# Squares of the residual added on GpSimd, one ones product in place of eight

## The chip, the cores and the metric

One core of a Trainium2 chip runs the whole program in one launch. The metric is the device time in microseconds, the median of repeated runs. The tensor engine (PE in the profile, its weight loads PEld), VectorE (DVE), ScalarE (ACT), GpSimd (POOL) and the DMA queue of SyncE (SP) run side by side and meet at semaphores.

## The reference

A residual x of 256 tokens by 1024 features, float32, goes through ten stages. Each takes a normed copy of x, puts it through a mixer or a feed-forward network, and adds the outcome to x:

```python
def rms_norm(x, gain):
    xf = x.astype(jnp.float32)
    y = xf * lax.rsqrt(jnp.mean(xf * xf, axis=-1, keepdims=True) + NORM_EPS)
    return (y * gain.astype(jnp.float32)).astype(x.dtype)
...
    for l in range(DEPTH):
        h = rms_norm(x, attn_norm[l])
        x = x + hybrid_mixer(h, ...)
        h = rms_norm(x, ffn_norm[l])
        x = x + conv_ffn(h, ...)
```

The first block above has two layers, so four stages: hybrid, ffn1, hybrid, ffn1. The second block has six: ffn2, a short convolution, ffn2, ffn2, a gated delta rule, ffn2. In those six the outcome of a stage is normed as well before it is added: `h = h + rms_norm_2(mix, g[3])`. The mean of squares over the 1024 features of each token, at the head of every stage, is what this case is about.

## The kernel before

**Layout.** Features lie on the 128 partitions: x is one SBUF tile `x` of 128 x 8 x 256, eight feature tiles (`KT`) of 256 tokens each. All weights come as 623 panels of 128x1024 float32, from HBM through a ring of six buffers `raw` (SyncE's queue). ScalarE rounds each panel to `whi` (line 762), VectorE subtracts to get the low part `wlo` (L1113), and the tensor engine makes each float32 product from three: high by high, high by low, low by high (`mm3`, L1701 to L1703). x is split in the same way to `xhi` (ScalarE, L778) and `xlo` (VectorE, L1124). Each panel is one call of `up` or `down`: 24 such products of 256 columns.

**Between two stages** everything goes tile by tile over k = 0 to 7. VectorE's `finish` updates x: from a bank in one operation where the stage has no norm behind it (L1152 after a hybrid, L1159 after ffn1), in two where it has (a scaled copy `tmp` from the bank, L1155, and `x<-x,tmp`, L1157). Two tiles behind it, it makes the `xlo` of the next stage (`prepare_tile`). ScalarE's `prepare` squares each tile to one of four buffers `sq` (L777) and makes its `xhi`; from the fifth tile on it waits with each square until the buffer has been read. The tensor engine's `up` is called with `prepare` for the first panel of a stage: for each k it waits for `xlo`, runs the three products, waits for the square and runs the ones product (L1721). This product, a matrix of ones by `sq` in plain float32, adds over the partitions and broadcasts the sum to all of them; the eight accumulate in `bank[6]`. In the delta stage that panel is the one of the gates.

**Behind the eighth ones product** VectorE takes mean and epsilon (`ms`, L1131), ScalarE the root (L781), VectorE the reciprocal (`rstd`, L1133). `rstd` is applied to the results of the panels, so the tensor engine needn't wait for it: it has two panels ready at the boundary, three where the stage has a norm behind it (`lead`). Further panels are split by VectorE only after `rstd`.

**GpSimd** does little. In stage 0 it issues ten loads (L681 and L686: tables, masks, and the small weights `w_in`, `pos_in`, `gate_w_in`), in stage 2 it issues four of them again as soon as stage 0 has released the space, and it has some products in the hybrid (L711, L714) and delta stages (L731, L737, L746). VectorE waits for the small weights before the copy at L1293, at the second tile of a hybrid stage. `third` is a pair of 128x256 buffers for the blocks of a stage, free at the boundaries.

Of the kernel before, what the change touches and what calls it, by code (L numbers as in the profile page):

```python
# [6 lines left out]
S = 256  # L7
KT = D // P
# [9 lines left out]
ALU = mybir.AluOpType  # L18
# [261 lines left out]
def build(nc, stages, arrays):  # L280
# [14 lines left out]
    with ExitStack() as ctx:  # L295
        def sb(name, shape, dt=F32):
            return ctx.enter_context(nc.sbuf_tensor(name, shape, dt))

        def sem(name):
            return ctx.enter_context(nc.semaphore(name))  # L300

        bank = [ctx.enter_context(nc.psum_tensor(f"bank{i}", [P, 512], F32)) for i in range(8)]
# [8 lines left out]
        ones = sb("ones", [P, P])  # L311
# [3 lines left out]
        sq = sb("sq", [P, 4, S])  # L315
# [7 lines left out]
        first = sb("first", [P, 2, S + 2])  # L323
        second = sb("second", [P, 2, S])
        third = sb("third", [P, 2, S])
        conv = sb("conv", [P, 2, S])
        act_out = sb("act_out", [P, 2, S])
        h = sb("h", [P, 2, S])
# [142 lines left out]
        xhi_ready = sem("xhi_ready")  # L471
        xlo_ready = sem("xlo_ready")
        sum_ready = sem("sum_ready")
        ms_ready = sem("ms_ready")
        root_ready = sem("root_ready")
        rstd_ready = sem("rstd_ready")
# [186 lines left out]
        def _(pool):  # L663
# [5 lines left out]
            def hybrid(s):  # L669
# [32 lines left out]
                for li in range(NL - 1):  # L702
# [9 lines left out]
                    if li == 0:  # L712

                        pool.tensor_tensor(level_k[0], gqk[:, 2:4, :], decay_, ALU.mult).then_inc(y["qe_ready"], 1)  # L714

            for s in range(n_stages):
                if stages[s][0] == HYBRID:
                    hybrid(s)
                if stages[s][0] != DELTA:
# [32 lines left out]
        def _(act):  # L752
# [16 lines left out]
            def prepare(s):  # L769

                for k in range(KT):
                    n = s * KT + k
                    wait_x(act, s, k)
                    if n >= 4:

                        act.wait_ge(sum_ready, n - 3)
                    act.activation(sq[:, n % 4, :], x[:, k, :], ACT.Square).then_inc(sq_ready, 1)  # L777
                    act.activation(xhi[:, k, :], x[:, k, :], ACT.Copy, scale=col(("pre", s), k)) \  # L778
                        .then_inc(xhi_ready, 1)
                act.wait_ge(ms_ready, s + 1)  # L780
                act.activation(rt[:], ms[:], ACT.Sqrt).then_inc(root_ready, 1)  # L781
# [317 lines left out]
        def _(dve):  # L1099
# [27 lines left out]

            def prepare_rstd(s):

                dve.wait_ge(sum_ready, KT * (s + 1))  # L1130
                dve.tensor_scalar(ms[:], bank[6][:, S:2 * S], 1.0 / D, EPS, ALU.mult, ALU.add).then_inc(ms_ready, 1)  # L1131
                dve.wait_ge(root_ready, s + 1)
                dve.reciprocal(rstd[:], rt[:]).then_inc(rstd_ready, 1)  # L1133
                dve.wait_ge(rstd_ready, s + 1)
# [563 lines left out]
        def _(pe):  # L1698
# [6 lines left out]
            def up(s, p, turn, dst, prepare=None):  # L1705

                slot = p % RING

                pe.wait_ge(lo_done, used(p, turn))
                for k in range(KT):  # L1710
                    if prepare is not None:

                        pe.wait_ge(xlo_ready, prepare * KT + k + 1)
                    last = mm3(dst, whi[slot][:, k * P:(k + 1) * P], wlo[slot][:, k * P:(k + 1) * P],
                               xhi[:, k, :], xlo[:, k, :], k == 0, k == KT - 1)
                    if k == KT - 1:
                        last.then_inc(panel_used, 1)
                    if prepare is not None:
                        n = prepare * KT + k
                        pe.wait_ge(sq_ready, n + 1)  # L1720
                        pe.matmul(bank[6][:, S:2 * S], ones[:], sq[:, n % 4, :], start=(k == 0), stop=(k == KT - 1),  # L1721
                                  skip_group_check=True).then_inc(sum_ready, 1)

            def down(s, f, p, turn):

# [496 lines left out]
```

## Time and profile before

| | us |
|---|---|
| median of 3 timed runs | 2488.87 (2486.8 to 2492.01) |
| span of the profiled execution, first to last instruction | 2484.9 |
| tensor engine busy | 2270.0 |
| weight loads busy | 2202.7 |
| VectorE busy | 1552.0 |
| ScalarE busy | 1107.8 |
| GpSimd busy | 76.6 |
| mean granted clock of the tensor engine | 0.958 |

The profile is of one execution, of which only the span is known; the median of the timed runs is 4.0 us above it. Weight loads overlap the products. A matmul's duration in the profile overlaps that of its neighbours, so the pace of a stream is read from starts. The granted clock is 1 at 2.4 GHz and 0.5 at 1.2 GHz.

### The profile page before, as it was taken

The page shows a single profiled execution, that of the slowest core. Times are in us where ns is not written, and L with a number is a line of the kernel's source. Part 1 is how long each engine was busy: PE and PEld are TensorE (multiplying, and loading weights), DVE is VectorE, ACT ScalarE, POOL GpSimd, SP SyncE. Part 2 cuts the span into 40 slices and gives each one's busy share as a digit, 9 for nine tenths or more (in the row PEclk, how much of TensorE's full clock was granted, in tenths as well). Part 3 has the DMA queues.
Part 4 walks back from the last instruction along what each step waited for, and adds up shares of the span by engine and source line. Part 5 has one row for each costly group of instructions (what it writes and reads, how often), then busy time and mean ns, then how long its engine had stood idle before and what let it go on. Part 6 is the DMA issues. An engine that isn't in the chain of part 4 may idle for free.

```text
span 2484.9 us, 46837 instructions
## 1 busy us (share of the span) xinstructions
PE 2270.0 (91%) x18150; PEld 2202.7 (89%) x18150; DVE 1552.0 (62%) x2543; ACT 1107.8 (45%) x1762; POOL 76.6 (3%) x84
## 2 busy tenths in 40 slices
PE   7998999999999999999898998998586877898997
PEld 6978999989789999999898998998576876898997
DVE  4456777754577777665677656665575655566665
ACT  4443455544444555544445445444424233245443
POOL 1002000000020000000000000000011010000000
PEclk9899999998999999999999999999788989999999
DMA  7432455543324455555354553553211111053552
GB/s 233 141 102 85 152 190 196 184 130 108 101 87 153 164 191 185 170 178 191 129 189 144 177 189 128 191 186 127 83 37 51 35 52 43 1 170 127 198 182 76
DMA packets 92186, 339.06 MB, mean 136 GB/s; under 512 B 10672, under 2 KB 10872, under 8 KB 91552
## 3 DMA queue, kind: packets, MB, share of 16 engines
q1 hardware_dynamic: 90288, 329.61, 39.7%
q0 software_dynamic: 1776, 7.73, 1.2%
q8 instruction: 89, 1.46, 0.2%
q14 instruction: 33, 0.27, 0.0%
HBM read 334.67 MB, written 2.62 MB: 136 GB/s over the span
## 4 chain that ended last, share of the span: by engine, by line
PE 79%; DVE 12%; ACT 6%; issue 3%; POOL 0%; DMA 0%; DVEq 0%; SPq 0%; ACTq 0%; POOLq 0%
PE bank L1701 22%; PE bank L1703 21%; PE bank L1702 21%; PE bank L2065 6%; DVE wlo L1113 3%; ACT whi L762 2%; DVE conv L1501 2%; PE bank L1721 1%; PE bank L1851 1%; PE bank L1777 1%; DVE arena L1285 1%; DVE tmp L1155 1%; ACT conv L968 1%; PE bank L1911 1%; DVE prstd L1145 0%
## 5 line engine op out<-in xcount | busy, mean ns | idle before, releaser
L1701 PE MATMUL bank<-xhi,whi 128*128 128x256 f32 x3496 | 1023.4, 293 | 82.9 <-DVE xlo L1124 50.7
L1702 PE MATMUL bank<-xlo,whi 128*128 128x256 f32 x3496 | 992.2, 284 | 0.0
L1703 PE MATMUL bank<-xhi,wlo 128*128 128x256 f32 x3496 | 991.6, 284 | 0.0
L1113 DVE TENSOR_TENSOR wlo<-raw,whi 128x1024 fp32r<-128x1024 f32 x623 | 741.4, 1231 | 245.5 <-ACT whi L762 245.1
L1701 PEld LDWEIGHTS bank<-xhi,whi 128*128 128x128 f32 x3496 | 674.4, 193 | 103.2 <-issue 66.7
L1702 PEld LDWEIGHTS bank<-xlo,whi 128*128 128x128 f32 x3496 | 674.1, 193 | 3.0
L1703 PEld LDWEIGHTS bank<-xhi,wlo 128*128 128x128 f32 x3496 | 671.9, 192 | 0.0
L762 ACT ACTIVATE whi<-raw 128x1024 fp32r<-128x1024 f32 x623 | 622.8, 1046 | 53.1 <-DVE arena L1282 21.6
L1701 PE MATMUL bank<-hhi,whi 128*128 128x256 f32 x1376 | 391.8, 285 | 7.1 <-DVE hlo L1234 5.6
L1703 PE MATMUL bank<-hhi,wlo 128*128 128x256 f32 x1376 | 390.3, 284 | 0.0
L1702 PE MATMUL bank<-hlo,whi 128*128 128x256 f32 x1376 | 390.0, 283 | 0.0
L1701 PEld LDWEIGHTS bank<-hhi,whi 128*128 128x128 f32 x1376 | 263.7, 192 | 8.8 <-issue 8.8
L1703 PEld LDWEIGHTS bank<-hhi,wlo 128*128 128x128 f32 x1376 | 264.0, 192 | 0.0
L1702 PEld LDWEIGHTS bank<-hlo,whi 128*128 128x128 f32 x1376 | 263.9, 192 | 0.0
L803 ACT ACTIVATE act_out<-first 128x256 f32<-128x256 f32 x104 | 43.6, 419 | 392.5 <-DVE first L1213 349.0
L2065 PE MATMUL bank<-arena 128*128 128x128 f32 x1184 | 147.9, 284 | 29.2 <-ACT arena L1027 14.5
L2065 PEld LDWEIGHTS bank<-arena 128*128 128x128 f32 x1184 | 141.6, 198 | 35.0 <-ACT arena L1027 15.7
L1213 DVE TENSOR_TENSOR first<-bank,rstd 128x256 f32<-128x256 f32 x132 | 55.8, 423 | 177.3 <-PE bank L1703 176.9
L821 ACT ACTIVATE hhi<-h 128x256 fp32r<-128x256 f32 x172 | 71.9, 418 | 146.8 <-DVE h L1232 92.9
L1234 DVE TENSOR_TENSOR hlo<-h,hhi 128x256 fp32r<-128x256 f32 x156 | 66.3, 425 | 75.5 <-ACT hhi L821 75.5
L1232 DVE TENSOR_TENSOR h<-act_out,second 128x256 f32<-128x256 f32 x148 | 63.0, 426 | 42.4 <-ACT act_out L812 21.6
L871 ACT ACTIVATE arena<-arena 128x256 f32<-128x256 f32 x48 | 20.0, 417 | 136.7 <-DVE arena L1285 136.7
(320 smaller groups left out, 1950.5 us busy)
## 6 DMA issues: line engine op xcount, KB each, us to landing
raw<-panels SPq DMA_DIRECT2D x623, 512.0 KB, 4.2
arena<-w_in POOLq DMA_DIRECT2D x2, 2048.0 KB, 10.6
bias_table<-arena POOLq DMA_DIRECT2D x1, 1536.0 KB, 34.1
x<-x_in SPq DMA_DIRECT2D x1, 1024.0 KB, 4.9
arena<-bias_table POOLq DMA_DIRECT2D x1, 1024.0 KB, 9.9
out<-x SPq DMA_DIRECT2D x1, 1024.0 KB, 3.9
masks<-masks_in SPq DMA_DIRECT2D x1, 576.0 KB, 6.0
arena<-level_masks_in POOLq DMA_DIRECT2D x1, 512.0 KB, 7.6
```

What stands on the lines that cost most here:

```text
L762: act.activation(whi[slot][:], raw[slot][:], ACT.Copy).then_inc(hi_done, 1)
L803: act.activation(act_out[:, sl, :], first[:, sl, 2:], ACT.Silu).then_inc(act_done, 1)
L821: act.activation(hhi[:, sl, :], h[:, sl, :], ACT.Copy).then_inc(hhi_done, 1)
L1113: dve.tensor_tensor(wlo[slot][:], raw[slot][:], whi[slot][:].bitcast(F32), ALU.subtract) \
L1213: dve.tensor_tensor(first[:, sl, 2:], pair[:, 0:S], rstd[:], ALU.mult).then_inc(gate_scaled, 1)
L1232: dve.tensor_tensor(h[:, sl, :], gated[:, sl, :], second[:, sl, :], ALU.mult).then_inc(h_done, 1)
L1234: dve.tensor_tensor(hlo[:, sl, :], h[:, sl, :], hhi[:, sl, :].bitcast(F32), ALU.subtract) \
L1501: last = dve.scalar_tensor_tensor(out=conv[:, sl, :], in0=delta_in[:, sl, w:w + S], scalar=col(("tap", s), w * 4 * KH + t), in1=conv[:, sl ...
L1701: pe.matmul(dst, w_hi, a_hi, start=start, stop=False, skip_group_check=True)
L1702: pe.matmul(dst, w_hi, a_lo, start=False, stop=False, skip_group_check=True)
L1703: return pe.matmul(dst, w_lo, a_hi, start=False, stop=stop, skip_group_check=True)
L2065: last = pe.matmul(bank[out_bank][:, m * P:(m + 1) * P], lhs(m), rhs(m), start=True, stop=True)
```

## The change

GpSimd gets a function `add_squares`, which it runs at the head of its work for each stage: seven additions that sum the eight squares to `sq_sum`, the first half of `third`. Each waits for its square and for the addition before it, the first also for the ones product of the stage before. ScalarE's squares wait for these additions instead of for ones products. The tensor engine runs one ones product on the sum, after the 24 products of the first panel, and VectorE waits for that one.

```diff
+        sq_sum = third[:, 0, :]
...
+        added = sem("added")
...
+            def add_squares(s):
+
+                if s:
+                    pool.wait_ge(sum_ready, s)
+                for k in range(1, KT):
+                    pool.wait_ge(sq_ready, KT * s + k + 1)
+                    if k > 1:
+                        pool.wait_ge(added, (KT - 1) * s + k - 1)
+                    a = sq[:, 0, :] if k == 1 else sq_sum
+                    pool.tensor_tensor(sq_sum, a, sq[:, k % 4, :], ALU.add).then_inc(added, 1)
+
             for s in range(n_stages):
+                add_squares(s)
                 if stages[s][0] == HYBRID:
                     hybrid(s)
...
-                    if n >= 4:
-
-                        act.wait_ge(sum_ready, n - 3)
+                    if k >= 4:
+
+                        act.wait_ge(added, (KT - 1) * s + max(k - 4, 1))
+                    elif s:
+
+                        act.wait_ge(added, (KT - 1) * s)
                     act.activation(sq[:, n % 4, :], x[:, k, :], ACT.Square).then_inc(sq_ready, 1)
...
-                dve.wait_ge(sum_ready, KT * (s + 1))
+                dve.wait_ge(sum_ready, s + 1)
...
-                    if prepare is not None:
-                        n = prepare * KT + k
-                        pe.wait_ge(sq_ready, n + 1)
-                        pe.matmul(bank[6][:, S:2 * S], ones[:], sq[:, n % 4, :], start=(k == 0), stop=(k == KT - 1),
-                                  skip_group_check=True).then_inc(sum_ready, 1)
+                if prepare is not None:
+
+                    pe.wait_ge(added, (KT - 1) * (prepare + 1))
+                    pe.matmul(bank[6][:, S:2 * S], ones[:], sq_sum, start=True, stop=True,
+                              skip_group_check=True).then_inc(sum_ready, 1)
```

GpSimd's order at the start of the program, before (loads are marked DMA; the semaphore waited for stands in brackets):

```order
L664 MEMSET ones 128x128
L665 MEMSET first 128x2x2
L681 DMA rel_table<-rel_in 32x8 [waits masks_loaded]
L681 DMA arena<-onehot_in 32x384
L681 DMA arena<-masked_in 8x384
L681 DMA arena<-level_masks_in 128x1024
L681 DMA arena<-cmp_masks_in 128x240
L681 DMA halves<-halves_in 128x2
L686 DMA arena<-w_in 128x4096
L686 DMA arena<-w_in 128x128
L686 DMA arena<-pos_in 128x32
L686 DMA arena<-gate_w_in 16x256
```

and with the change, whose lines are shifted by 2:

```order
L666 MEMSET ones 128x128
L667 MEMSET first 128x2x2
L727 ISA
L727 TENSOR_TENSOR third<-sq 128x256 [waits sq_ready,masks_loaded]
L727 TENSOR_TENSOR third<-third,sq 128x256 [waits added,sq_ready] x6
L683 DMA rel_table<-rel_in 32x8
L683 DMA arena<-onehot_in 32x384
L683 DMA arena<-masked_in 8x384
L683 DMA arena<-level_masks_in 128x1024
L683 DMA arena<-cmp_masks_in 128x240
L683 DMA halves<-halves_in 128x2
L688 DMA arena<-w_in 128x4096
```

The seven additions stand ahead of all ten loads. In stage 2 the four loads of L686 also stand behind that stage's additions now, where they had followed stage 0's products directly.

The tensor engine's first panel of a stage before, its first three tiles:

```order
L1701 MATMUL bank<-xhi,whi 128x256 [waits lo_done,xlo_ready,masks_loaded,consts_ready]
L1702 MATMUL bank<-xlo,whi 128x256
L1703 MATMUL bank<-xhi,wlo 128x256
L1721 MATMUL bank<-sq,ones 128x256 [waits sq_ready]
L1701 MATMUL bank<-xhi,whi 128x256 [waits xlo_ready]
L1702 MATMUL bank<-xlo,whi 128x256
L1703 MATMUL bank<-xhi,wlo 128x256
L1721 MATMUL bank<-sq,ones 128x256 [waits sq_ready]
```

and with the change:

```order
L1718 MATMUL bank<-xhi,whi 128x256 [waits lo_done,xlo_ready,masks_loaded,consts_ready]
L1719 MATMUL bank<-xlo,whi 128x256
L1720 MATMUL bank<-xhi,wlo 128x256
L1718 MATMUL bank<-xhi,whi 128x256 [waits xlo_ready]
L1719 MATMUL bank<-xlo,whi 128x256
L1720 MATMUL bank<-xhi,wlo 128x256
```

The ones product and its wait are gone from between the triples; one of each stands behind the eighth.

## Rows read from the trace of the kernel before

**Rows 1.** The page: busy time, share and instructions of each engine.
```profile
PE 2270.0 (91%) x18150; PEld 2202.7 (89%) x18150; DVE 1552.0 (62%) x2543; ACT 1107.8 (45%) x1762; POOL 76.6 (3%) x84
```
**Rows 2.** View of line 1721, the ones products: durations in ns, first and last start.
```profile
L1721 PE MATMUL bank<-sq,ones x160: 377/379/634, 15.3 to 2282.6; 128*128 128x256 f32 x160
```
**Rows 3.** Timeline of PE, stage 1: start, us, idle before and its releaser.
```profile
320.31 0.60 PE L1721 MATMUL bank<-sq,ones 128*128 128x256 f32 x2
...
321.10 0.59 PE L1721 MATMUL bank<-sq,ones 128*128 128x256 f32 x2
...
325.82 0.59 PE L1721 MATMUL bank<-sq,ones 128*128 128x256 f32 x2
...
330.43 0.39 PE L1701 MATMUL bank<-xhi,whi 128*128 128x256 f32 x1 [1.19 <-DVE wlo L1113]
```
**Rows 4.** Timeline of DVE, the boundary into stage 1.
```profile
317.88 1.08 DVE L1152 SCALAR_TENSOR_TENSOR x<-bank,x 128x256 f32<-128x256 f32 x3
...
320.71 0.47 DVE L1124 SCALAR_TENSOR_TENSOR xlo<-x,cols,xhi 128x256 fp32r<-128x256 f32 x1
...
321.44 0.48 DVE L1124 SCALAR_TENSOR_TENSOR xlo<-x,cols,xhi 128x256 fp32r<-128x256 f32 x1
...
324.28 0.48 DVE L1124 SCALAR_TENSOR_TENSOR xlo<-x,cols,xhi 128x256 fp32r<-128x256 f32 x1 [0.28 <-ACT xhi L778]
326.45 0.42 DVE L1131 TENSOR_SCALAR ms<-bank 128x256 f32<-128x256 f32 x1 [1.69 <-PE bank L1721]
```
**Rows 5.** Timeline of PE, the first panel of stage 5.
```profile
1214.41 0.55 PE L1701 MATMUL bank<-xhi,whi 128*128 128x256 f32 x1 [5.93 <-DVE xlo L1124]
...
1222.66 0.59 PE L1721 MATMUL bank<-sq,ones 128*128 128x256 f32 x2
```
**Rows 6.** Timeline of DVE, the boundary into stage 5.
```profile
1216.29 0.48 DVE L1124 SCALAR_TENSOR_TENSOR xlo<-x,cols,xhi 128x256 fp32r<-128x256 f32 x1
...
1217.54 0.48 DVE L1124 SCALAR_TENSOR_TENSOR xlo<-x,cols,xhi 128x256 fp32r<-128x256 f32 x1
...
1221.10 0.48 DVE L1124 SCALAR_TENSOR_TENSOR xlo<-x,cols,xhi 128x256 fp32r<-128x256 f32 x1 [0.18 <-ACT xhi L778]
1223.29 0.42 DVE L1131 TENSOR_SCALAR ms<-bank 128x256 f32<-128x256 f32 x1 [1.71 <-PE bank L1721]
```
**Rows 7.** Line 737 in ns; POOL and DVE near 1817; the page's L1113.
```profile
L737 POOL TENSOR_TENSOR arena<-tmp,arena x16: 724/1171/1707, 1816.5 to 2114.6; 128x256 f32<-128x256 f32 x16
...
1817.47 1.17 POOL L737 TENSOR_TENSOR arena<-tmp,arena 128x256 f32<-128x256 f32 x1
...
1816.85 2.34 DVE L1620 TENSOR_TENSOR arena<-arena,masks 128x512 f32<-128x512 f32 x2
1819.12 1.75 DVE L1113 TENSOR_TENSOR wlo<-raw,whi 128x1024 fp32r<-128x1024 f32 x1
...
L1113 DVE TENSOR_TENSOR wlo<-raw,whi 128x1024 fp32r<-128x1024 f32 x623 | 741.4, 1231 | 245.5 <-ACT whi L762 245.1
```
**Rows 8.** Windows: stretch, us; busy PE (x), others; PEclk, DMA share, GB/s.
```profile
1214.40:1218.70 4.30, 4.29 (x16) 3.85 (x16) 4.16 (x11) 2.77 (x7) 0.00 (x0) 0.50 0.02 4
...
1223.00:1229.00 6.00, 6.00 (x52) 5.97 (x51) 5.19 (x5) 4.22 (x5) 0.00 (x0) 1.00 0.08 21
...
1823.50:1828.50 5.00, 3.30 (x15) 0.50 0.03 13
```
**Rows 9.** The start: POOL, ACT and DVE; L686's loads, min/median/max to landing.
```profile
8.02 0.69 POOL L681 DMA_DIRECT2D rel_table<-rel_in  x1 [7.02 <-DMA masks<-masks_in]
...
11.35 1.06 POOL L686 DMA_DIRECT2D arena<-w_in  x2
...
13.01 0.40 ACT L777 ACTIVATE sq<-x 128x256 f32<-128x256 f32 x1
...
31.10 0.66 DVE L1293 COPY arena<-tmp 128x240 f32<-128x240 f32 x2
...
DMA to landing us min/median/max: 7.8/10.5/12.9
```

## The prediction

> **What bounds the kernel now.** I read the page's busy line first. The tensor engine is busy for 2270.0 of 2484.9 us and GpSimd for 76.6 us [rows 1]: one engine bounds, and another is nearly free. The view of the line with the ones products comes next. Its 160 records are 80 products, since a plain float32 product leaves two records [rows 2]. Then I read the timelines of two of the ten places where a stage prepares its residual, because every product that goes stands there.
>
> Stage 1 stands for stages 1 to 4, which follow a stage without a norm behind it. The ones products start every 0.79 us (320.31, 321.10), the last at 325.82 [rows 3]. A dense triple takes 0.35 us, three times 6.00/51 [rows 8], so one ones product costs 0.44 us. VectorE makes the low parts xlo at a faster pace, one in 0.73 us (320.71, 321.44); the last ends at 324.76 and the mean square starts at 326.45, 1.69 us later [rows 4]. Here the tensor engine is the slower of the two, by little. Afterwards it waits for VectorE again, 1.19 us at 330.43 [rows 3].
>
> Stage 5 stands for stages 5 to 9, which follow a stage with a norm behind it. VectorE needs 1.25 us per tile (1216.29, 1217.54), its last xlo ends at 1221.58, and the mean square starts at 1223.29, 1.71 us later [rows 6]. The tensor engine came out of 5.93 us of idleness [rows 5], and its granted clock was 0.50 for the first 4.3 us of this work, 1.2 of 2.4 GHz [rows 8]. VectorE sets the pace, and the ones products fill time that the tensor engine would wait out.
>
> **What goes.** 70 of 80 products at 0.44 us are 31 us of tensor time. On the path lies only what the engine trails behind xlo. With the ones products out of the loop, the mean square would follow the last xlo by a triple, one ones product and some 0.25 us of handing over: 1.04 us at full clock instead of 1.7, or 1.8 us at half clock (0.70 + 0.88 + 0.25).
>
> **What comes: seven adds on GpSimd.** The nearest row is its multiply of 128x256 tiles: 0.72 us at best, median 1.17, at most 1.71 [rows 7]. A chain of seven with a wait of some 0.06 us each takes 5.5 us undisturbed, 8.6 us at the median. It cannot end before the last square, but where squares come every 1.25 us it keeps up.
>
> The dearer part is what these adds do to VectorE. Around 1817 both engines work on pairs of SBUF tiles, and they alternate: each GpSimd multiply takes 1.17 us, and two VectorE operations take 2.34 us [rows 7]. The split of a panel right behind them took 1.75 us against a mean of 1.23 [rows 7], so one GpSimd operation held it up by 0.52 us; I take 0.55. The Trainium skill, "SBUF — State Buffer", section "Who interferes with whom", says that the second of the two engines is blocked for the whole instruction of the first, and only if VectorE reads two SBUF tiles; with 0.72 us per block the term for stages 5 to 9 below would be 0.54 us per tile and the sum some 5 us more.
>
> In stages 1 to 4 the xlo operation reads x and xhi, two SBUF tiles; the update reads a bank and can run under an add. The cycle becomes 0.55 + 0.33 = 0.88 us instead of 0.73: over seven tiles the last xlo is **1.1 us** later. The adds, in step with it, end earlier. In stages 5 to 9 an add meets two such operations per tile (x<-x,tmp and xlo), and hides only the 0.18 us or so by which it overlaps the scaled copy from the bank: 0.37 us more per tile, six times, **2.2 us**. Both bounds are open: 0 if nothing is blocked, 0.55 for each of eight tiles (4.4 us) if every add blocks in full.
>
> **The clock.** Around 1826 the tensor engine was busy for 3.30 of 5.00 us at half clock and was not granted more [rows 8]. In stages 5 to 9 a triple at half clock (0.70 us) now falls into a cycle of some 1.6 us, without the ones products between them, so I expect half clock until the dense work begins with the last triple. If the return takes 4.3 us as above, 1.5 us of it is priced in the 1.8 us above, and the other 2.8 us does half of its work: **1.4 us** lost, since the engine has panels ready there (0.9 to 2.5 by how the return falls). In stages 1 to 4 a full-clock triple fills 0.35 of 0.88 us, and the clock may fall too. Then the handing over takes 1.8 us instead of 1.7, and the next panel is slower by more than the 1.19 us wait hides; together 0.2 us. The Trainium skill, "TensorE: Matmul & The Clock Gate", Part 1, calls the throttled clock the default, which activity releases; so it speaks against taking filler products away.
>
> **The start.** GpSimd's queue now has the seven adds ahead of its ten loads. The second square is there at 13.41 [rows 9]; seven adds at 0.88 us end near 19.7. Six loads take 3.3 us to issue (8.02 to 11.35), so w_in is issued near 23.0 and its three followers by 24.6. With 7.8 to 12.9 us to landing, all are there at 32.4 to 37.5. VectorE needs them for the copy that stands at 31.10 [rows 9]. The mean square itself comes earlier by 1 to 2 us, as squares no longer wait for ones products, but this wait eats it. VectorE's next splits and reads stand behind the wait, and the tensor engine behind them. I take the early landing, since the panels' own first rush is over by then: **+1.5 us** (-1.5 to +6). For stage 2 the loads are issued near 522 instead of 314. With 7.9 us they land just before the copy at 531; I cost this at nothing, and 3 us if landing takes 12.9.
>
> **Sum.** Stages 1 to 4: 1.1 + 0.2 = 1.3, four times 5.2. Stages 5, 6, 7, 9: 2.2 + 1.4 = 3.6, four times 14.4. Stage 8: 2.2, the tensor engine waits for VectorE there afterwards in any case. The start: 1.5. Together +23.3. The profiled span is 2484.9 and the median of the timed runs 2488.87, so 4.0 lies around it: 2484.9 + 23.3 + 4.0 = **2512 us**, 0.9% slower. The chance is 0.50.
>
> **Rivals.**
> 1. GpSimd's chain is the bound, at its median of 1.17 us plus the wait. In stages 1 to 4 seven adds end 8.6 us after the second square instead of 6.2, which makes the mean square 1.6 us later still (four times: 6.4), and the start 2.4 us later. 2512 + 8.8 = 2521. For it: the median is what it needs beside a busy VectorE. Against it: VectorE's pairs here are 256 wide, those at 1817 were 512. 0.20.
> 2. The loads are late, 12.9 us to landing at the start and at stage 2: 4.5 + 3 more, 2520. 0.10.
> 3. The blocking is small, and only the clock bites: without the 1.1 and 2.2 us, stages 1 to 4 give about nothing, four of the others 1.4, the start 1.5: +7, 2496. Against it stands the split of 1.75 us. 0.12.
> 4. The other side: neither blocking nor clock. Then the mean square comes 0.65 us earlier at nine places, and the start gains 1.5: -7.4, 2481. It decides once the last xlo slips by less than 0.65 us and the clock is full by the last triple. The clock speaks against it: with less work between idle gaps it would have to return sooner. 0.03.
> 5. Gains and losses cancel to within 0.2%, which is 5 us and about what a measurement can tell from no change: parts of 3 and 4 mixed. 0.05.
>
> **How the numbers follow.** The range runs from rival 3 at its low end to rival 1 together with late loads: 2496 to 2532. Outside it are rivals 4 and 5, and mishaps above. Faster 0.03, same 0.09 (rival 5 and the low third of rival 3), slower 0.88.
>
> **What would show it.** VectorE's x<-x,tmp and xlo operations, now 0.42 and 0.48 us, must show longer ones while adds run, and the last xlo of stage 5 must end 12 to 13 us after the first update instead of 10.4. Granted clock 0.50 until behind the ones product there. A wait before the copy of the start. If xlo keeps its pace, the first term falls; if the clock returns as before, the 1.4 us falls; if the tensor engine waits for GpSimd behind the last triple, rival 1 holds. A time under 2494 would make the whole argument wrong.

## The result and the profile after

| | before | changed |
|---|---|---|
| median of the timed runs | 2489.74 us (2486.8 to 2492.01, 4 runs) | 2515.97 us (2513.16 to 2518.97, 4 runs) |
| span of the profiled execution | 2484.9 | 2511.4 |
| mean granted clock | 0.958 | 0.942 |

The ratio is 1.0102, with an interval of 1.0086 to 1.0117: 26.2 us slower. In a later set of runs on another chip it was 1.0088 (1.0074 to 1.0103), some 22 us.

The page's busy line of the changed kernel, as [rows 1]:

```profile
PE 2281.7 (91%) x18010; PEld 2207.5 (88%) x18010; DVE 1572.5 (63%) x2543; ACT 1108.3 (44%) x1762; POOL 129.1 (5%) x154
```

140 matmul records are gone, and yet the tensor engine is busy 11.7 us longer: the rest runs at a colder clock. GpSimd has 70 operations and 52.5 us more. VectorE has not one operation more and is busy 20.5 us longer. The views of the adds, of the update behind a norm and of xlo, in ns (min/median/max), first and last start, forms:

```profile
L727 POOL TENSOR_TENSOR third<-third,sq x60: 725/732/858, 14.9 to 2305.4; 128x256 f32<-128x256 f32 x60
...
L1174 DVE TENSOR_TENSOR x<-x,tmp x48: 424/438/721, 1217.0 to 2506.7; 128x256 f32<-128x256 f32 x48
...
L1141 DVE SCALAR_TENSOR_TENSOR xlo<-x,cols,xhi x80: 472/617/953, 14.1 to 2305.8; 128x256 fp32r<-128x256 f32 x80
```

The adds run at 0.73 us. The two VectorE operations that read two SBUF tiles have stretched: the update was never over 0.43 us before, and xlo had a median of 0.48. The operations that read one bank and one SBUF tile kept their 0.41 and 0.48 us. The adds themselves, six of stage 3:

```profile
818.17 5.11 POOL L727 TENSOR_TENSOR third<-third,sq 128x256 f32<-128x256 f32 x6
```

They start every 0.876 us ((5.11 - 0.73)/5): 0.73 us of add and 0.14 us of handing over from each to the next, with no wait for a square.

**Stage 1**, the timeline of DVE in the changed kernel, answers to [rows 4]:

```profile
318.83 0.42 DVE L1169 SCALAR_TENSOR_TENSOR x<-bank,x 128x256 f32<-128x256 f32 x1
319.16 0.62 DVE L1141 SCALAR_TENSOR_TENSOR xlo<-x,cols,xhi 128x256 fp32r<-128x256 f32 x1
319.70 0.41 DVE L1169 SCALAR_TENSOR_TENSOR x<-bank,x 128x256 f32<-128x256 f32 x1
320.04 0.62 DVE L1141 SCALAR_TENSOR_TENSOR xlo<-x,cols,xhi 128x256 fp32r<-128x256 f32 x1
...
322.67 1.88 DVE L1141 SCALAR_TENSOR_TENSOR xlo<-x,cols,xhi 128x256 fp32r<-128x256 f32 x3
326.51 0.42 DVE L1148 TENSOR_SCALAR ms<-bank 128x256 f32<-128x256 f32 x1 [1.97 <-PE bank L1738]
```

xlo starts every 0.88 us (319.16, 320.04) where it was 0.73, the pace of the adds. Each is issued while an add runs and ends some 0.28 us after it. In stages 2 to 4 the last two, with no update between them, take 0.95 us each. The wait behind the last one is 1.97 us, not 1.69. The timeline of PE there answers to [rows 3]:

```profile
319.38 0.28 PE L1720 MATMUL bank<-xhi,wlo 128*128 128x256 f32 x1
...
320.71 0.58 PE L1718 MATMUL bank<-xhi,whi 128*128 128x256 f32 x1 [0.26 <-DVE xlo L1141]
321.10 0.41 PE L1719 MATMUL bank<-xlo,whi 128*128 128x256 f32 x1
...
325.42 1.05 PE L1738 MATMUL bank<-third,ones 128*128 128x256 f32 x2
```

After two or three triples with gaps between them a product takes 0.41 us instead of 0.28, half clock, and so does the one ones product.

**Stage 5**, the timelines of POOL and of DVE, the latter for [rows 6]:

```profile
1221.43 0.74 POOL L727 TENSOR_TENSOR third<-third,sq 128x256 f32<-128x256 f32 x1 [0.81 <-ACT sq L794]
1222.97 0.74 POOL L727 TENSOR_TENSOR third<-third,sq 128x256 f32<-128x256 f32 x1 [0.81 <-ACT sq L794]
```

```profile
1221.22 0.47 DVE L1172 SCALAR_TENSOR_TENSOR tmp<-bank,cols,prstd 128x256 f32<-128x256 f32 x1
1221.72 0.72 DVE L1174 TENSOR_TENSOR x<-x,tmp 128x256 f32<-128x256 f32 x1
1222.37 0.47 DVE L1141 SCALAR_TENSOR_TENSOR xlo<-x,cols,xhi 128x256 fp32r<-128x256 f32 x1
...
1228.04 0.71 DVE L1141 SCALAR_TENSOR_TENSOR xlo<-x,cols,xhi 128x256 fp32r<-128x256 f32 x1 [0.16 <-ACT xhi L795]
1230.71 0.42 DVE L1148 TENSOR_SCALAR ms<-bank 128x256 f32<-128x256 f32 x1 [1.96 <-PE bank L1738]
```

The add of 1221.43 ends at 1222.17; the update issued at 1221.72 ends 0.27 us after that, 0.30 us late. The xlo behind it meets no add and takes 0.47. That is so for the four tiles in the middle; the first and the last xlo meet an add and take 0.95 and 0.71 us, so 0.47 + 4 x 0.30 + 0.23 makes the 1.9 us by which the last xlo is late. The windows of the changed kernel (busy time of PE, PEld, DVE, ACT and POOL, PEclk, DMA share, GB/s), as [rows 8]:

```profile
1220.00:1228.00 8.00, 5.47 (x17) 4.03 (x18) 7.71 (x17) 4.09 (x11) 3.95 (x6) 0.50 0.00 0
1228.50:1234.50 6.00, 6.00 (x38) 5.82 (x37) 3.52 (x4) 3.33 (x5) 0.00 (x0) 0.72 0.00 0
```

Half clock lasts through the loop and well into the dense work behind it.

**Where the time went**, by stage, in us, worked out from the start of the first update, the end of the last xlo, and the starts of the mean square and of the next stage's first update; changed less before, profile against profile:

| stage | to the last xlo | from there to the mean square | from there to the next stage | sum |
|---|---|---|---|---|
| 0 (hybrid) | -0.22 | +0.52 | -1.13 | -0.8 |
| 1 | +0.61 | +0.28 | 0.00 | +0.9 |
| 2 (hybrid) | +1.08 | +0.27 | +1.28 | +2.6 |
| 3 | +1.09 | +0.27 | 0.00 | +1.4 |
| 4 | +1.07 | +0.24 | -0.07 | +1.2 |
| 5 | +1.87 | +0.25 | +0.44 | +2.6 |
| 6 | +1.86 | +0.27 | +0.59 | +2.7 |
| 7 | +1.88 | +0.28 | +1.24 | +3.4 |
| 8 (delta) | +1.65 | +0.27 | +7.37 | +9.3 |
| 9 | +1.88 | +0.28 | +1.05 | +3.2 |

Together 26.5. The 7.37 us in the delta stage stand where no line of the change does.

### The profile page after: what moved, and what is told of

Its sections match the earlier page's. It is cut to its first block, busy times and chain, and to the rows that moved or that the text cites. A ratio compares the mean times of both kernels' runs of the same rounds, so it can differ in the third digit from the quotient of the medians.

```text
span 2511.4 us, 46697 instructions
## 1 busy us (share of the span) xinstructions
PE 2281.7 (91%) x18010; PEld 2207.5 (88%) x18010; DVE 1572.5 (63%) x2543; ACT 1108.3 (44%) x1762; POOL 129.1 (5%) x154
## 4 chain that ended last, share of the span: by engine, by line
PE 78%; DVE 13%; ACT 5%; issue 3%; POOL 0%; DMA 0%; DVEq 0%; SPq 0%; ACTq 0%; POOLq 0%
PE bank L1718 22%; PE bank L1719 21%; PE bank L1720 21%; PE bank L2082 6%; DVE wlo L1130 3%; ACT whi L776 2%; DVE conv L1518 2%; DVE xlo L1141 1%; PE bank L1868 1%; PE bank L1794 1%; DVE tmp L1172 1%; DVE arena L1302 1%; ACT conv L985 1%; PE bank L1928 1%; PE bank L2199 0%
## 5 line engine op out<-in xcount | busy, mean ns | idle before, releaser
L1719 PE MATMUL bank<-xlo,whi 128*128 128x256 f32 x3496 | 1002.4, 287 | 0.0
L1718 PEld LDWEIGHTS bank<-xhi,whi 128*128 128x128 f32 x3496 | 682.7, 195 | 127.8 <-issue 69.5
L1719 PEld LDWEIGHTS bank<-xlo,whi 128*128 128x128 f32 x3496 | 685.3, 196 | 1.0
L1720 PEld LDWEIGHTS bank<-xhi,wlo 128*128 128x128 f32 x3496 | 682.6, 195 | 0.0
L2082 PEld LDWEIGHTS bank<-arena 128*128 128x128 f32 x1184 | 143.3, 200 | 34.9 <-ACT arena L1044 15.7
L727 POOL TENSOR_TENSOR third<-sq 128x256 f32<-128x256 f32 x10 | 8.1, 814 | 1419.8 <-ACT sq L794 1419.8
```

Of the source, the lines that this page charges most:

```text
L1718: pe.matmul(dst, w_hi, a_hi, start=start, stop=False, skip_group_check=True)
L1719: pe.matmul(dst, w_hi, a_lo, start=False, stop=False, skip_group_check=True)
L1720: return pe.matmul(dst, w_lo, a_hi, start=False, stop=stop, skip_group_check=True)
L2082: last = pe.matmul(bank[out_bank][:, m * P:(m + 1) * P], lhs(m), rhs(m), start=True, stop=True)
```

## The experiments

Nine other kernels ran, and the two once more. "Table" below means the same division by stage, against before's first profile.

**The adds alone**: all eight ones products stay, and GpSimd sums the squares for nobody.

```diff
+            for s in range(n_stages):
+                add_squares(s)
...
+                dve.wait_ge(added, (KT - 1) * (s + 1))
```

> The kernel before with the seven GpSimd adds put in, whose sum nobody reads; the eight ones products stay in the loop. Blocking theory: the last xlo ends 8.0 us after the first update at stages 1 to 4 (before: 6.9) and 12.2 us at stages 5 to 9 (before: 10.35), with the ones products the tensor engine stays at full clock, so the mean square follows the last xlo by 1.0 to 1.1 us instead of 1.7; net +0.4 us at four places and +1.2 us at five, about +8 us in all, 2498. Rival, only the lost ones products cost (clock): the same time as before, 2490, and xlo at its old pace. Rival, GpSimd's chain is late: no effect here either, since nobody waits for its end.

Measured: 2513.31 us, ratio 1.0073 (1.0054 to 1.0092), 19 us for the 8 expected. The last xlo is 1.08 us later in stages 2 to 4, 0.62 in stage 1 and 1.84 to 1.88 in stages 5 to 9 but for the delta stage's 1.62: the changed kernel's own numbers. Its stage 5, DVE:

```profile
1228.60 0.71 DVE L1176 TENSOR_TENSOR x<-x,tmp 128x256 f32<-128x256 f32 x1
...
1237.05 0.42 DVE L1150 TENSOR_SCALAR ms<-bank 128x256 f32<-128x256 f32 x1 [1.45 <-PE bank L1740]
```

So the blocking is GpSimd's work and nothing else of the change. The wait behind the last xlo is shorter than before (1.45 for 1.71), since the tensor engine has caught up: at half clock a triple and a ones product need 1.58 us (0.70 + 0.88), far more than the 1.25 us per tile of before and hardly more than the 1.545 here; and the dense work behind it has lost at most 0.3 us. All that its table has up to the mean squares is 10.7 us; the time is higher than that, and in the profile a further 15.7 us lie behind the mean squares of stages 0, 2 and 8 (3.7, 5.6 and 6.4), of which more below.

**One product and no adds**: the tensor side of the change without GpSimd. It leaves out the squares of seven tiles; the eighth's sum is scaled by eight.

```diff
-                dve.wait_ge(sum_ready, KT * (s + 1))
-                dve.tensor_scalar(ms[:], bank[6][:, S:2 * S], 1.0 / D, EPS, ALU.mult, ALU.add).then_inc(ms_ready, 1)
+                dve.wait_ge(sum_ready, s + 1)
+                dve.tensor_scalar(ms[:], bank[6][:, S:2 * S], KT / D, EPS, ALU.mult, ALU.add).then_inc(ms_ready, 1)
...
+                    pe.wait_ge(sq_ready, KT * (prepare + 1))
+                    pe.matmul(bank[6][:, S:2 * S], ones[:], sq[:, 3, :], start=True, stop=True,
+                              skip_group_check=True).then_inc(sum_ready, 1)
```

> The kernel before with one ones product of the last square instead of eight and no adds at all (the other seven squares are left out of the sum, which is scaled by eight). Blocking theory: xlo keeps 6.9 and 10.35 us. Clock theory: at stages 5 to 9 the granted clock stays 0.5 until behind the ones product, the mean square follows the last xlo by 1.9 to 2.0 us instead of 1.7, and 0.4 to 1.2 us more are lost behind it, +5 us over the five places; at stages 1 to 4 the triples come every 0.73 us and the clock may hold, then the mean square comes 0.6 us earlier, otherwise 0.3 us later: 2488 to 2496 in all. Rival, the removed products are pure gain: 0.65 us earlier at nine places, 2483.

Measured: 2491.64 us, ratio 0.9991 (0.9981 to 1.0001). This is about what the change would have brought, had the adds been free. Its mean squares of stages 3 and 5, DVE:

```profile
819.61 0.42 DVE L1132 TENSOR_SCALAR ms<-bank 128x256 f32<-128x256 f32 x1 [1.15 <-PE bank L1722]
...
1221.14 0.42 DVE L1132 TENSOR_SCALAR ms<-bank 128x256 f32<-128x256 f32 x1 [2.19 <-PE bank L1722]
```

In stage 3 the wait is 1.15 us, a gain of 0.53: the clock fell in the loop (0.51 from 815.0 to 818.5) but was full again for the ones product (1.00 from 818.6 on). In stage 5 it is 2.19, a loss of 0.5 to the half clock, and the panels behind lose another 0.3 to 0.7 us. Over stages 1, 3 and 4 that gives -2.0 us, over 5, 6, 7 and 9 it gives +4.1. So 31 us less tensor work are worth nothing that can be measured: rival 4's gain is real where the clock is full by the ones product, and the clock takes it back where it isn't.

**The changed kernel with fillers**: behind the triples of tiles 0 to 6 the tensor engine runs a product of ones and x that nobody reads.

```diff
+                    elif prepare is not None:
+                        pe.matmul(bank[6][:, S:2 * S], ones[:], x[:, k, :], start=True, stop=True,
+                                  skip_group_check=True)
```

> The changed kernel with seven filler products of the old size (ones by x, thrown away) between the triples, so the tensor engine does the old work and GpSimd the new. Clock theory: the granted clock at the boundaries is as before (none below full at stages 1, 3, 4), the mean square follows the last xlo by 1.0 to 1.3 us instead of 1.96, nothing is lost behind it: 8 to 12 us less than the changed kernel, 2504 to 2508, with xlo still at 8.0 and 12.2 us by the blocking theory. Rival, removing the products was a gain that blocking outweighed: putting them back costs 0 to 3 us, 2516 to 2519.

Measured: 2504.97 us, ratio 1.0046 (1.0030 to 1.0062), 11 us under the changed kernel (which has 2516.19 in the next run, on the same chip, with its loads moved), with seven useless products per stage. In its table the seven stages other than 0, 2 and 8 are 7.0 us shorter than in the changed kernel: the last xlo is where it was, the wait behind it is 1.15 to 1.46 us, and the panels behind lose 0.3 us at most. The window of 15 us from 0.1 us behind the mean square of stage 7 shows it, first for the changed kernel and then for this one:

```profile
1547.00:1562.00 15.00, 15.00 (x120) 15.00 (x120) 11.96 (x16) 10.07 (x14) 0.00 (x0) 0.92 0.51 170
```

```profile
1551.30:1566.30 15.00, 15.00 (x130) 15.00 (x129) 11.96 (x16) 10.04 (x14) 0.00 (x0) 1.00 0.49 166
```

The same stretch holds 130 products instead of 120. (The Trainium skill, "TensorE: Matmul & The Clock Gate", Part 1, has the gate open with activity: by that rule the fillers bring the clock back, and the trace agrees.) The profiled execution is the slowest of its five, 2513.04 us, with a span as long as the changed kernel's; the 4 us beyond the seven stages lie in executions that no profile shows.

**The loads ahead of the adds**: `add_squares` of a hybrid stage moved behind GpSimd's loads.

```diff
                     pool.dma_start(dst, arrays[name][layer]).then_inc(y["small_loaded"], 16)
+                add_squares(s)
```

> The changed kernel with the loads of each hybrid stage issued ahead of that stage's adds, as before the change. The copy of the gains on VectorE, which took 1.84 us behind the moved memsets and cast of GpSimd against 0.17, takes 0.17 again: 1.7 us less at the start, 2514. If the loads' landing mattered too, stage 2 gives another 1.3 us back. Rival, the order of GpSimd's loads is indifferent: 2516.

Measured: 2516.19 us, ratio 1.0088 (1.0069 to 1.0107). The copy of the gains takes 0.17 us again and the copy of the start stands at 31.06, as expected, but an interval of some 5 us to either side doesn't tell 2514 from 2516. Stage 2 behind its mean square is 1.28 us over before here too, so that isn't the loads. In this profile the clock of stage 2 was full by the ones product, and the mean square came 1.14 us behind the last xlo instead of 1.96.

**Memsets for adds**: as the adds alone, but GpSimd writes and reads nothing.

```diff
-                    pool.tensor_tensor(sq_sum, a, sq[:, k % 4, :], ALU.add).then_inc(added, 1)
+                    pool.memset(third[:, :, :], 1.0).then_inc(added, 1)
```

> The kernel before, with its eight ones-products, and beside them on GpSimd, at the places and behind the waits of the changed kernel's adds, 70 memsets of the same 128x256 f32 tile: GpSimd writes SBUF there but reads nothing. If VectorE's two-input instructions are blocked by GpSimd's reads alone, xlo stays at 0.48 us (0.62 us in the changed kernel), the stretch from the first update to the last xlo stays at 6.9 and 10.35 us, and the time is that of the kernel before (ratio 0.999 to 1.001). Rival: any GpSimd instruction on SBUF blocks them. Then xlo is at 0.62 us, the stretches grow by 1.1 and 1.9 us as with the adds alone, and the time is 14 to 19 us over before (ratio 1.006 to 1.0075).

Measured: 2497.44 us, ratio 1.0022 (1.0011 to 1.0032). The kernel before itself had 1.0016 beside it (below), so this is its time. Both halves of `third` are written, 128x512 in 0.52 us, where the expectation has one. Its views of xlo and of the memsets:

```profile
L1142 DVE SCALAR_TENSOR_TENSOR xlo<-x,cols,xhi x80: 471/477/487, 13.8 to 2290.9; 128x256 fp32r<-128x256 f32 x80
...
L727 POOL MEMSET third<- x70: 524/525/528, 13.4 to 2290.5; 128x512 f32 x70
```

Not one of 80 xlo operations was held, nor one of 48 updates (0.43 us at most), though 65 of these 128 started while a memset ran; and the table has 0.00 to 0.03 us up to the last xlo in stages 1 to 7. It is GpSimd's reading that blocks, as the Trainium skill has it ("SBUF — State Buffer", "Who interferes with whom": a VectorE instruction with two SBUF inputs contends with a GpSimd one that reads SBUF, not with one that only writes).

**Before, profiled again.**

> The kernel before, profiled a second time. The time must be that of the kernel before. What is asked is how far its own profile repeats: in the first one the last stage but one took 532.6 us from its mean square to the next stage's first update, and 103 us of it at half clock; the four profiles of changed kernels have 537 to 540 us and 123 to 126 us there, the kernel with one product of eight and no adds among them, whose code in that stretch is that of before. If those 5 to 7 us are how the clock happens to fall in one execution, this profile gives 535 to 540 us and its span is 5 to 8 us over the first one's 2484.9. If they belong to the change, it gives 532 to 533 us and a span of 2484 to 2487. The stretches that the prediction counted, 6.9 us (stages 1 to 4) and 10.35 us (stages 5 to 9) from the first update to the last xlo, must repeat within 0.1 us by either.

Measured: 2497.19 us against 2492.51 of the runs beside it, ratio 1.0016 (1.0005 to 1.0027) for one and the same kernel, so intervals here are some 0.1% too narrow. Its span was 2490.1. The delta stage from the mean square to the next stage's first update, in before's second profile, in the memset kernel and in the changed kernel (windows, columns as above; the first profile's is 532.6 long with PEclk 0.90):

```profile
1739.21:2275.59 536.38, 432.60 (x3276) 416.85 (x3274) 315.59 (x539) 191.72 (x329) 37.03 (x40) 0.89 0.20 64
```

```profile
1741.26:2281.07 539.81, 435.61 (x3276) 419.47 (x3274) 315.75 (x539) 191.70 (x329) 37.06 (x40) 0.89 0.19 64
```

```profile
1754.30:2294.29 539.99, 435.98 (x3276) 420.02 (x3274) 315.89 (x539) 191.76 (x329) 37.08 (x40) 0.88 0.19 64
```

The instructions are the same and VectorE's busy time is within 0.3 us, and the stretch varies by over 7 us with the clock: half clock lasted 103 us in the first profile, 120 in the second and 126 in the changed kernel. The 535 to 540 us and the longer span held; the stretches up to the last xlo repeated within 0.02 us in stages 1 to 7, but stage 9's took 10.9 us and not 10.35. Part of the first pair's 26.5 us was before's short delta stage.

**The changed kernel again.**

> The changed kernel once more, on the chip of these runs, beside the kernel before in five rounds. The kernel before, profiled a second time, had a span 5.2 us over its first one, 4.2 us of it in the two hybrid stages and the delta stage, where no line of the change stands. So the change is worth less than the 26.5 us between the first two profiles: the sum by stages without those three stretches gives 21 to 22 us, ratio 1.0080 to 1.0095. If the whole 26 us are the change's, the ratio is 1.0100 to 1.0115 again. The stretch from the first update to the last xlo must be 8.0 us (stages 2 to 4) and 12.2 us (5 to 9) again, and half clock beside the mean square 6.8 us (stages 1 to 4) and 13.7 to 17.1 us (5 to 9).

Measured: 2517.51 us, ratio 1.0088 (1.0074 to 1.0103), as expected without those three stretches. Its span was 2519.0, 7.6 over its first profile's, of which 4.4 lie in stage 0 and 2.8 in stage 2; each stage from 3 to 9 is within 0.25 us of the first profile. So the division by stage is firm where no hybrid or delta mixer runs, and those mixers scatter.

**The ones product ahead of the triple.** No GpSimd: each tile's ones product only moves ahead of its triple, since its square is there before xlo.

```diff
                     if prepare is not None:
+                        n = prepare * KT + k
+                        pe.wait_ge(sq_ready, n + 1)
+                        pe.matmul(bank[6][:, S:2 * S], ones[:], sq[:, n % 4, :], start=(k == 0), stop=(k == KT - 1),
+                                  skip_group_check=True).then_inc(sum_ready, 1)
                         pe.wait_ge(xlo_ready, prepare * KT + k + 1)
```

> The kernel before with each tile's ones-product ahead of the triple of the same tile in TensorE's order, nothing else. The ones-product needs the square, which ScalarE has made while VectorE still makes xlo, so the last tile's triple (0.33 us at full clock) no longer stands ahead of the mean square. The path's theory: the trail from the last xlo to the mean square falls from 1.7 to 1.3 us or less at the nine places, and the time by 2 to 4 us (ratio 0.9985 to 0.9992). Rival: the triples only move behind it and the normalisation finds TensorE later, so that the time is that of before within 1 us.

Measured: 2494.26 us, ratio 0.9999 (0.9986 to 1.0013). The wait behind the last xlo fell by 0.7 to 0.8 us at eight of nine places, more than expected, and the panels behind lost 0.4 us in stages 6, 7 and 9. Stages 1, 3, 4, 5, 6, 7 and 9 together are 3.9 us shorter, and that does not stand out of the scatter of the others: the 2 to 4 us expected don't show in the time.

**The same in a single pass.** Squares and ones in float32r, the type of `xhi` and `whi`, of which a dense product takes 0.12 us (a third of 0.35) where a plain float32 one costs 0.44; its 80 ones products leave 80 records instead of 160. There are two buffers for the squares, and to make room `rt` shares the buffer of `ms`, and `prstd` that of `rstd`.

```diff
-                        pe.matmul(bank[6][:, S:2 * S], ones[:], sq[:, n % 4, :], start=(k == 0), stop=(k == KT - 1),
+                        pe.matmul(bank[6][:, S:2 * S], ones_r[:], sq_r[:, n % 2, :], start=(k == 0), stop=(k == KT - 1),
```

> The squares are written in float32r and the ones-product of each tile is one pass (0.11 us at full clock in place of 0.44), placed ahead of the tile's triple; no work on GpSimd. It wants what the change wants, a lighter trail behind the last xlo, without the adds. The path's theory: the trail falls from 1.7 us to about 0.9 at stages 1 to 4 and the stretch before it stays at 6.9 and 10.35 us; nine times 0.7 is 6 us. The clock's theory: with 2.6 us less of TensorE's work in each prologue the clock falls there earlier, as in the changed kernel, and takes back up to 1 us at each of stages 5 to 9: 4 to 5 us. Together 0 to 6 us faster than before (ratio 0.9975 to 1.0). A third: the clock takes more than it gives, and the time is 2 to 6 us over before.

Measured: 2490.95 us, ratio 0.9992 (0.9981 to 1.0003). The wait fell by 1.0 us and more, but the last xlo came up to 0.9 us later, because with two buffers ScalarE waited for the tensor engine (15.1 us in all before the squares, 7.1 before).

**Four buffers for it.** The buffer `sq` itself becomes float32r, and is rounded in its other uses too.

```diff
-        sq = sb("sq", [P, 4, S])
+        sq_r = sb("sq_r", [P, 4, S], F32R)
+        sq = sq_r[:].bitcast(F32)
```

> The run before this one (ones-product in one pass, ahead of the triple, two buffers for the squares) lost up to 0.9 us per prologue because ScalarE waited for the ones-product before each square (0.3 to 0.9 us before L782). Here the squares have four float32r buffers again, as before; nothing else differs, but for four other uses of that buffer, which are rounded too. If that wait is all that held it, the stretch from the first update to the last xlo is 6.9 us at stages 1 to 4 (7.2 to 7.8 with two buffers) and 10.35 us at stages 5 to 9 (10.8), the trail stays at 0 to 0.65 us, and the time is 5 to 9 us under before (ratio 0.9964 to 0.998). Rival, the clock alone: TensorE has less to do in the prologue, falls to half clock after it for longer, and gives the gain back: ratio 0.998 to 1.0.

Measured: 2488.83 us against 2494.18, ratio 0.9975 (0.9961 to 0.9989): 5 to 6 us under the kernel before. The interval leaves out 1 by little, and before against itself had been 0.16% off, so the gain is probable and not shown by the time alone. ScalarE's wait for the tensor engine is gone, the last xlo is where it was (6.81 and 10.34 us), and the mean square of stage 3 comes 0.90 us behind it, DVE:

```profile
820.58 0.42 DVE L1136 TENSOR_SCALAR ms<-bank 128x256 f32<-128x256 f32 x1 [0.90 <-PE bank L1719]
```

The clock takes its part here too: in stages 6 and 7 the panels behind lose 1.4 us each. The time is at the low end of the expected 5 to 9 us; the wait behind the last xlo is 0.1 to 1.1 us, more than the 0.65 expected, where the clock is down.

**Fillers for that kernel**, as above, behind the triples of tiles 0 to 5, in the other half of the bank. They disturb the running sum, so the sum that it norms by isn't the reference's.

> The kernel of the run e8, with a four-pass product of ones and x without a reader (0.44 us at full clock) behind the triples of tiles 0 to 5 of each prologue, so that TensorE has about as much to do there as before and none of it stands behind the last xlo. If the clock takes a part of e8's gain, half clock beside the mean square of stages 5 to 9 comes back from 10 to 14 us to 6.8 us, and the time is 2 to 5 us under e8's, ratio 0.994 to 0.997 to before. If the clock takes nothing, or the fillers stand in the way of the ones-products, it is e8's time or 1 to 4 us over it.

Measured: 2499.47 us, ratio 1.0020 (1.0012 to 1.0029). Half clock did not spread in any stage, and the panels behind lost 0.4 us instead of 1.4, but the wait behind the last xlo was 1.1 to 1.8 us in all stages but 9, as the fillers stood ahead of the ones products. Neither case of the expectation foresaw 11 us over the kernel without fillers. The profiles differ by 2.2 us only, as this one is the fastest of its eleven executions, 5.9 us under the median; they don't show where the rest lies.

## Why the prediction was right, point by point

| term | predicted | measured, profile against profile |
|---|---|---|
| blocking, stages 1 to 4 | 1.1 each, 4.4 | 0.61, 1.08, 1.09, 1.07: 3.9 |
| handing over there | 0.2 each, 0.8 | 0.24 to 0.28: 1.1 |
| blocking, stages 5 to 9 | 2.2 each, 11.0 | 1.65 to 1.88: 9.1 |
| clock, stages 5, 6, 7, 9 (handing over and behind it) | 1.4 each, 5.6 | 0.69, 0.86, 1.52, 1.33: 4.4 |
| delta stage behind the last xlo | 0 | +7.6 |
| start | +1.5 | -0.8 |
| stage 2 behind its mean square (its loads) | 0 | +1.3 |
| sum | 23.3 | 26.5 |

**The two blocking terms came near, the first by luck.** In stages 1 to 4 the cycle is 0.88 us, as worked out, but not for the reason given. The sum put a hold-up of 0.55 us in the place of xlo's own 0.40 (0.73 less 0.33); on top of it, the cycle would be 1.28 us. Measured, an add holds such an xlo by 0.14 us (0.62 for 0.48), and the 0.88 us are the pace of GpSimd's chain: adds of 0.73 us with 0.14 between them, where the prediction had a wait of 0.06. Of the 1.08 us in stages 2 to 4 this pace makes 0.6, and the last xlo, held by 0.47, the rest. That the chain sets the pace is read from the trace; no run changed the add's length alone.

In stages 5 to 9 the step "an add meets two such operations per tile" was wrong: in the middle tiles it meets one, the update, and has ended before xlo. It holds that one for 0.30 us, and a tile's cycle grew from 1.25 to 1.545 us, not by 0.37. The Trainium skill's rule that the prediction set beside it ("SBUF — State Buffer", "Who interferes with whom"), with 0.72 us per block, is right about who blocks whom; but an add here starts before the update does, so only what was left of it was waited out.

**The clock term** was right in kind and about a quarter too large: 1.1 us in the mean for the 1.4, between 0.7 and 1.5. Half clock lasted 0.9 to 2.4 us behind the mean square of these stages, not 2.8, and the panels lost about half of that; in stages 1 to 4 it ended within 1.3 us, and in stages 1, 3 and 4 nothing was lost behind it. The handing over at half clock took the 1.8 us of triple, ones product and handing over, plus 0.15. The reading that VectorE sets the pace in stage 5 before holds at full clock only: at half clock the tensor engine's 1.58 us per tile are more than VectorE's 1.25, and so it trails by 1.7 us.

**The start** failed in its path, though the copy is late by about as much as was forecast. The loads did go behind the adds, as said:

```profile
14.92 5.10 POOL L727 TENSOR_TENSOR third<-third,sq 128x256 f32<-128x256 f32 x6
19.96 0.70 POOL L683 DMA_DIRECT2D rel_table<-rel_in  x1
...
23.31 1.06 POOL L688 DMA_DIRECT2D arena<-w_in  x2
```

That is what was forecast to 0.3 us. But no wait for them appears before the copy, now L1310, so w_in landed within 9.8 us (23.31 to 33.06). The copy is nevertheless 1.96 us later than its 31.10. What held it stands higher up on VectorE:

```profile
25.58 1.84 DVE L1280 COPY qk_gain<-cols 128x8 f32<-128x8 f32 x1
...
33.06 0.66 DVE L1310 COPY arena<-tmp 128x240 f32<-128x240 f32 x2
```

and the last section says why. The wait that was forecast does exist where this hold-up is small. In the adds alone, whose loads are issued 1.5 us later and whose `qk_gain` takes 0.43 us, the copy waits for the last of them, as it does with the memsets (2.18 us):

```profile
35.09 0.65 DVE L1312 COPY arena<-tmp 128x240 f32<-128x240 f32 x2 [2.04 <-DMA arena<-gate_w_in]
```

What a late copy costs isn't told by these runs: stage 0 came out 0.8 us shorter with the change and 3.6 longer in its second profile, and moving the loads back shows nothing in the time within 5 us.

**The delta stage** was off by the most, and this stays open. Three profiles of kernels with the change's adds and one product have 540 us there and two of the kernel before have 533 and 536; but the six kernels without adds have 535 to 541. Whether the change moves that stage at all isn't told by these runs. Without the rests of the three stages with a mixer the table sums to 19.0 us, where the prediction had 21.8 for the same places.

**The 4.0 us around the span** were no cost of starting and ending. The profiled execution took 2513.16 us as timed for a span of 2511.4, 1.75 apart. The rest is that a span of 2484.9 belongs to the fastest of before's executions, 2486.8. Taken right, the sum would have been made against the median in the same way, so the total isn't touched.

**The rivals.** GpSimd's chain did not delay the ones product: the adds ran at 0.73, not at 1.17 us, and in each stage the last one ended before the last triple did (in stage 5 at 1228.47, before the last xlo). In stages 1 to 4 it did bound VectorE, as told above, at a pace that this rival didn't have. Late loads: by no more than the forecast itself. Small blocking: refuted by the adds alone. The other side, a gain of 0.65 us at each place, appears only without adds and with the clock full by the ones product: 0.6 to 0.7 us up to the mean square in stages 1 to 4. The upper end of the range doesn't follow from its own terms: rival 1 with late loads is 2512 + 8.8 + 7.5 = 2528, not 2532.

**The total.** The forecast difference of 23.3 us lies between the 22 and the 26 us measured. The mechanisms behind 19.0 us of the measured are seen stage by stage; that the total is so close is in part luck, since 1.5 us of the forecast and 7.5 us of the first pair of profiles lie in the stages with a mixer, where a kernel differs from itself by several us.

## What to carry to other kernels

Work moved to GpSimd isn't free for VectorE: if it reads SBUF beside VectorE instructions with two SBUF inputs, each meeting costs up to what is left of GpSimd's instruction, and a chain of such instructions can force its own pace on VectorE. Look at whose pace sets the stretch before moving work there. Taking products away from a stretch in which the tensor engine waits between them gave no time here and cost some by the clock. What counts is what stands behind the last input: independent products put ahead of the dependent ones cut that wait by 0.7 to 0.8 us, and only with cheaper products as well did the time move, by 0.25%, not much more than the 0.16% by which one kernel differed from itself. Before a difference in a stage far from the change is explained, profile the unchanged kernel twice.

## What the runs showed of the hardware

**A copy of 128x8 held for 1.7 us.** `qk_gain`, one SBUF input, takes 0.17 us before. In the changed kernel it took 1.84 (25.58 to 27.42), while GpSimd's queue, later than before, ran these:

```profile
25.41 1.01 POOL L691 MEMSET arena<- 128x512 f32 x2
...
26.34 1.05 POOL L694 CAST arena<-arena 128x1024 uint8<-128x1024 f32 x1
```

It ended 0.03 us after the cast (27.39). Had the memsets not held it, it would have been over before the cast began at 26.34. The second profile has the same (1.81 us, ending 0.03 us after the cast), the one with fillers too (1.36 us, 0.03 us), and with the loads ahead of the adds it is back at 0.17. So a copy, unlike the xlo operations, is held by memsets as well, and several GpSimd instructions can pass ahead of it. The Trainium skill ("SBUF — State Buffer", "Who interferes with whom") says that copies can enter a mode that needs the shared port pair and are then fully blocked; the trace agrees.

**Length without cause in the program.** The three stretches with a hybrid or delta mixer differ from one execution to another by up to 6.5, 5.7 and 8 us in the thirteen profiles (292.5 to 299.0, 290.2 to 295.9, 532.6 to 540.6) with the same VectorE and ScalarE instructions in them, and roughly in step with the clock: half clock lasted 27 us in the shortest first stretch and 41 in the longest. Whether the clock makes the length or follows it isn't shown. The dense panels behind the mean squares of stages 1, 3 and 4 took the same time in all of them within 0.2 us.
